# The residual's identity matmuls go first in each output tile of the gated mixer

## The chip, the cores and the metric

One core of one Trainium2 chip runs the whole program in one launch. The metric is the device time in microseconds of an execution; of several executions the median counts.

## What the kernel must compute

One inference step through two layers, for 1,024 prompt tokens and 64 sample tokens (8 sequences of 8), 1,088 tokens together. Layer 0 has a gated mixer in chunks of 128 tokens, layer 1 has sliding-window attention, and each is followed by a gated ConvFFN. The part that matters here is the end of the gated mixer with its residual:

```python
z = gelu(h @ w_in);  u, v = split(z);  v = layer_norm(v)
mixed = einsum('gts,bnsgc->bntgc', tril(w_s), v in chunks) + b_s
y = x + (u * mixed) @ w_out          # w_out is 2048 x 1024
```

Everything is f32. The kernel keeps activations with features on the 128 partitions and tokens along the free axis, so the residual x, which lies in memory by tokens, must be transposed where it is added.

## The kernel before, in words

All large products are computed from operands that are split in a high and a low part. A raw block of weights, `wraw`, is loaded by DMA from the SyncE queue (`load`, L295); ScalarE rounds it to `wh` (`hi`, L302), VectorE subtracts to get `wl` (`lo`, L306). Each of the three has two slots, s = 0 and s = 1. TensorE then does three products per block: weights high by activations high, high by low, low by high. `rows` (L323) does this for one block of 128 input features: nine matmuls, three products by three column chunks of 384, 384 and 320 tokens, which are added up in three PSUM banks. There are two such areas of three banks, A (banks 0 to 2) and B (banks 3 to 5); a tile m of an output uses area m % 2.

The gated mixer runs in three steps: v (`token_major`, L1734), u with the mixing matmuls (L323 and L1769), and the output projection, `out_tile`, which the change touches. The output projection has 8 tiles of 128 output features. A tile has 16 blocks `rows`, 8 on the weights of slot 0 and 8 on those of slot 1, on the gated product in its parts `gh` and `gl`. Between the two halves stands the residual: 9 matmuls in the program, one for each tile of tokens, whose stationary operand is the x of 128 tokens by 128 features, `xm`, and whose moving operand is the identity `idn`. So x comes out transposed and is added in PSUM to the sum. Both operands are f32, and each of these matmuls stands in the trace twice, 18 a tile, at L1788.

What orders the work around them:

- Semaphores alone, and the order in which each engine's program is written. TensorE waits on `free` (the area has been read out), on `w_lo` (the slot's weights are split), for tile 0 on `g_lo` before each block (that block of `gl` is there), and on `xm_in` (the residual's tile has landed). It signals `w_used` at the end of each half, on which the next split into that slot waits, and `xm_used` after the residual's matmuls, on which the next load of `xm` waits. There is one buffer `xm`.
- `gh` lies over the memory of the projections' input `hh` and `hl`, so ScalarE starts on it (L1181) only when TensorE has done the last u tile. VectorE first does the gating of the last group (L1439 to L1450) and then `gl` (L1468), 16 blocks, each after the `gh` of the block. Meanwhile TensorE does the last mixing matmuls (L1769) and comes to output tile 0.
- SyncE issues, for m = 0 to 6, the two weight loads of tile m + 1 (each waits for the split of the slot before), then waits for `xm_used` of tile m, and issues the two DMAs of `xm` for tile m + 1 (L988, L989).
- ScalarE, in each tile: the split of slot 0 for the next tile after the first half; after the second half the copy of the area to x (L1202), the split of slot 1, and the squares for the next norm (L1191), which GpSimd adds up (L1069).
- After tile 7 come the ConvFFN's first blocks (L323 on `hh`, `hl`), which wait for the scaled x in its two parts (L1212, L1484).

Of the kernel before, what the change touches and what calls it, by code (L numbers as in the profile page):

```python
# [12 lines left out]
TT = 9  # L13
# [65 lines left out]
def step_program(nc, x_prompt, x_sample, cache_swa_k, cache_swa_v, state_ffn_conv, mix_norm_g, sgu_w_in, sgu_ln_g,  # L79
# [7 lines left out]
    with ExitStack() as ctx:  # L87
        ctx.enter_context(nc.allow_non_contiguous_dma(reason="small vectors"))

        def sb(name, shape, dt=f32, stack=ctx):  # L90
            return stack.enter_context(nc.sbuf_tensor(name, shape, dt))

        def sem(name):
            return ctx.enter_context(nc.semaphore(name))


        idn = sb("idn", [128, 128])
# [6 lines left out]
        xm = sb("xm", [128, TT, 128])  # L104
# [108 lines left out]
        ps = ctx.enter_context(nc.psum_tensor("ps", [128, 8, 512], f32))  # L213
        BANK = (0, 3)
# [35 lines left out]
        g_hi, g_lo, xm_in, xm_used = sem("g_hi"), sem("g_lo"), sem("xm_in"), sem("xm_used")  # L250
# [38 lines left out]
        def at(c, m=0, i=None):  # L289
            return c if i is None else i * m + c  # L290
# [28 lines left out]
        def rows(pe, area, s, k, col, mov, start, stop):  # L319

            for n, (w, part) in enumerate(PARTS):
                for c, (c0, cn) in enumerate(CH):
                    ins = pe.matmul(ps[:, BANK[area] + c, 0:cn], w[:, s, col:col + 128], mov[part][:, k, c0:c0 + cn],  # L323
                                    start=start and n == 0, stop=stop and n == 2, skip_group_check=True)
            return ins
# [18 lines left out]
        x_mov, g_mov = (hh, hl), (gh, gl)  # L344
# [1315 lines left out]
        def _(pe):  # L1660
# [38 lines left out]
            for g in range(GROUPS):  # L1699
                ins = pe.transpose(ps[:, 5 + g // 4, (g % 4) * 128:(g % 4) * 128 + 128], wsr[:, g, :], idn[:, :])  # L1700
# [3 lines left out]
            for n in range(4):  # L1704
                ins = pe.transpose(ps[:, 7, 32 + 88 * n:120 + 88 * n], vecs[0:88, 1 + n, :], idn[0:88, 0:88])
# [45 lines left out]
            with pe.Fori(0, 8) as i:  # L1751
                for s in range(2):
# [5 lines left out]
                    for k in range(KT):  # L1758
                        ins = rows(pe, 0, s, k, 128 * k, x_mov, k == 0, k == 7)
# [3 lines left out]
                    for t in range(TT):  # L1763
                        n = 128 if t < 8 else 64
# [3 lines left out]
                        for r, (a, w) in enumerate(((vnh, src[0]), (vnh, src[1]), (vnl, src[0]))):  # L1768
                            ins = pe.matmul(o, a[:, t, :], w[:, gi, :].rearrange("p o n -> p (o n)"),  # L1769
                                            start=r == 0, stop=r == 2)  # L1770
# [3 lines left out]
            def out_tile(m, i=None):  # L1774
                area = m % 2
                pe.wait_ge(free[area], at((A_O, B_O)[area] + m // 2, 1, i))
                for s in range(2):
                    pe.wait_ge(w_lo, at(2 * (P_OUT + m) + s + 1, 4, i))
                    for k in range(8):
                        if m == 0:  # L1780
                            pe.wait_ge(g_lo, 8 * s + k + 1)
                        ins = rows(pe, area, s, 8 * s + k, 128 * k, g_mov, s == 0 and k == 0, s == 1 and k == 7)
                    ins.then_inc(w_used, 1)
                    if s == 0:
                        pe.wait_ge(xm_in, at(32 * (m + 1), 64, i))
                        for t in range(TT):
                            n = 128 if t < 8 else 64
                            ins = pe.matmul(ps[:, BANK[area] + t // 3, (t % 3) * 128:(t % 3) * 128 + n], xm[0:n, t, :],  # L1788
                                            idn[0:n, 0:n], start=False, stop=False, skip_group_check=True)
                        ins.then_inc(xm_used, 1)  # L1790

            by_pairs(pe, out_tile)

            def transpose_y(m):
# [100 lines left out]
            for m in range(KT):  # L1895
                ins = pe.transpose(ps[0:64, m // 4, (m % 4) * 128:(m % 4) * 128 + 128], x[:, m, SEQ:T], idn[:, :])
# [27 lines left out]
```

## Time and profile before

| | |
|---|---|
| three runs | 2893.01, 2893.94 (median), 2895.33 us |
| profiled execution, its time | 2889.9 us |
| profiled execution, its span | 2888.0 us |
| mean granted clock of TensorE | 0.971 |
| TensorE matmuls busy | 2765.0 us, 96% of the span |
| VectorE busy | 1500.1 us, 52% |
| ScalarE busy | 761.8 us, 26% |
| GpSimd busy | 158.3 us, 5% |
| DMA | 131.10 MB, mean 45 GB/s |

A granted clock of 1.00 is TensorE's upper level, 2.4 GHz; 0.50 is the lower, 1.2 GHz; a value between is a stretch with some of each. A matmul's duration in the trace is longer than its distance to the next, since they are pipelined: rates are read from starts.

### The profile page before, as it was taken

To read this page: it belongs to the slowest core of one execution; us is meant where nothing else is said; L and a number is where in the kernel's file an instruction comes from. 1 tells how busy PE (TensorE), PEld (TensorE's weight loads), DVE (VectorE), ACT (ScalarE), POOL (GpSimd) and SP (SyncE) were. 2 spreads that over 40 slices of the span, in tenths; PEclk is the share of its full clock that TensorE was granted. 3 is DMA by queue.
4 is the path that set the end of the run, shared out by engine and by line. 5 is a ranking of instruction groups with operands and counts; after the bars stand their busy time and mean duration, and the time that the engine had idled before them with its cause. 6 is when DMAs were issued, how large, how long until landed. Compare 5 with 4: busy or idle time off the path is not lost.

```text
span 2888.0 us, 44609 instructions
## 1 busy us (share of the span) xinstructions
PE 2765.0 (96%) x18002; PEld 2702.8 (94%) x18002; DVE 1500.1 (52%) x2168; ACT 761.8 (26%) x1219; POOL 158.3 (5%) x109
## 2 busy tenths in 40 slices
PE   8999999999999999999999967789999999999998
PEld 8999999998999999999998955479899999999998
DVE  5226666102655555555573299923555555555546
ACT  4112223112222222222233336512322222222221
POOL 0000000110000000000021043201100000000000
PEclk9999999999999999999999977879999999999999
DMA  4111111211111111111111100011111111111112
GB/s 139 38 54 46 40 46 55 63 57 45 41 42 45 45 45 45 45 45 44 41 39 52 36 35 1 20 30 37 38 45 44 39 43 45 45 45 45 45 45 70
DMA packets 192182, 131.10 MB, mean 45 GB/s; under 512 B 6132, under 2 KB 179020, under 8 KB 192076
## 3 DMA queue, kind: packets, MB, share of 16 engines
q1 hardware_dynamic: 181240, 124.26, 14.3%
q10 hardware_dynamic: 10868, 5.79, 0.7%
q8 instruction: 54, 0.88, 0.1%
q14 instruction: 20, 0.16, 0.0%
HBM read 123.85 MB, written 8.15 MB: 46 GB/s over the span
## 4 chain that ended last, share of the span: by engine, by line
PE 90%; DVE 6%; ACT 3%; issue 1%; DMA 0%; DVEq 0%; POOL 0%; SPq 0%; ACTq 0%; POOLq 0%
PE ps L323 71%; PE ps L1734 12%; PE ps L1769 2%; ACT pr L500 1%; PE ps L889 1%; PE ps L1681 1%; PE ps L1815 1%; DVE stt L655 1%; DVE hl L1484 1%; DVE sm L651 1%; PE ps L1788 1%; PE ps L906 0%; ACT sm L491 0%; PE ps L1822 0%; DVE x L1569 0%
## 5 line engine op out<-in xcount | busy, mean ns | idle before, releaser
L323 PE MATMUL ps<-hh,wh 128*128 128x384 f32 (+1 forms) x2688 | 598.8, 331 | 16.4 <-DVE hl L1484 9.1
L323 PE MATMUL ps<-hl,wh 128*128 128x384 f32 (+1 forms) x2688 | 595.2, 329 | 0.0
L323 PE MATMUL ps<-hh,wl 128*128 128x384 f32 (+1 forms) x2688 | 594.8, 329 | 0.0
L302 ACT ACTIVATE wh<-wraw 128x1024 fp32r<-128x1024 f32 x200 | 212.4, 1063 | 1193.0 <-PE ps L323 1056.3
L323 PEld LDWEIGHTS ps<-hh,wh 128*128 128x128 f32 x2688 | 459.7, 189 | 19.8 <-issue 10.8
L323 PEld LDWEIGHTS ps<-hh,wl 128*128 128x128 f32 x2688 | 461.5, 189 | 0.0
L323 PEld LDWEIGHTS ps<-hl,wh 128*128 128x128 f32 x2688 | 461.3, 189 | 0.0
L306 DVE TENSOR_TENSOR wl<-wraw,wh 128x1024 fp32r<-128x1024 f32 x200 | 247.7, 1239 | 390.6 <-ACT wh L302 389.0
L1509 DVE TENSOR_TENSOR a_sb<-ps,rbc 128x768 f32<-128x768 f32 x88 | 84.3, 958 | 556.7 <-PE ps L323 556.6
L1569 DVE TENSOR_TENSOR x<-x,ps 128x768 f32<-128x768 f32 x352 | 237.9, 717 | 99.3 <-PE ps L323 97.9
L1734 PE MATMUL ps<-wh,hh 128*128 128x256 f32 x936 | 267.5, 286 | 9.6 <-DVE x L1569 6.5
L1734 PE MATMUL ps<-wl,hh 128*128 128x256 f32 x936 | 266.3, 285 | 0.0
L1734 PE MATMUL ps<-wh,hl 128*128 128x256 f32 x936 | 266.2, 284 | 0.0
L323 PE MATMUL ps<-fh,wh 128*128 128x384 f32 (+1 forms) x1008 | 222.7, 329 | 4.5 <-DVE wl L306 4.5
L323 PE MATMUL ps<-fl,wh 128*128 128x384 f32 (+1 forms) x1008 | 222.6, 329 | 0.0
L323 PE MATMUL ps<-fh,wl 128*128 128x384 f32 (+1 forms) x1008 | 222.6, 328 | 0.0
L1734 PEld LDWEIGHTS ps<-wh,hh 128*128 128x128 f32 x936 | 181.2, 194 | 10.3 <-issue 6.7
L1734 PEld LDWEIGHTS ps<-wl,hh 128*128 128x128 f32 x936 | 181.3, 194 | 0.0
L1734 PEld LDWEIGHTS ps<-wh,hl 128*128 128x128 f32 x936 | 181.2, 194 | 0.0
L323 PEld LDWEIGHTS ps<-fh,wh 128*128 128x128 f32 x1008 | 171.8, 188 | 5.0 <-issue 5.0
L323 PEld LDWEIGHTS ps<-fh,wl 128*128 128x128 f32 x1008 | 172.7, 188 | 0.0
L323 PEld LDWEIGHTS ps<-fl,wh 128*128 128x128 f32 x1008 | 172.3, 188 | 0.0
(234 smaller groups left out, 3102.4 us busy)
## 6 DMA issues: line engine op xcount, KB each, us to landing
wraw<-in_ffn_w_up SPq DMA_DIRECT2D x88, 512.0 KB, 3.8
wraw<-in_ffn_w_down SPq DMA_DIRECT2D x44, 512.0 KB, 3.3
wraw<-in_sgu_w_in SPq DMA_DIRECT2D x32, 512.0 KB, 4.5
wraw<-in_sgu_w_out SPq DMA_DIRECT2D x16, 512.0 KB, 4.0
wraw<-in_attn_w_qkv SPq DMA_DIRECT2D x12, 512.0 KB, 3.6
xin<-in_x_prompt SPq DMA_DIRECT2D x8, 512.0 KB, 9.6
xm<-in_x_prompt SPq DMA_DIRECT2D x8, 512.0 KB, 3.7
wraw<-in_attn_w_o SPq DMA_DIRECT2D x8, 512.0 KB, 3.9
```

Of the source, the lines that this page charges most:

```text
L302: act.activation(wh[:, s, :], wraw[:, s, :], ACT.Copy).then_inc(w_hi, 1)
L306: dve.tensor_tensor(wl[:, s, :], wraw[:, s, :], wh[:, s, :].bitcast(f32), sub).then_inc(w_lo, 1)
L323: ins = pe.matmul(ps[:, BANK[area] + c, 0:cn], w[:, s, col:col + 128], mov[part][:, k, c0:c0 + cn], start=start and n == 0, stop=stop and ...
L500: act.activation(pr[:, z, 128 * h:128 * h + 128], sm[:, z, 128 * h:128 * h + 128], ACT.Exp, bias=stt[:, 8 * z + h:8 * z + h + 1], scale=HD ...
L651: ins = dve.copy_predicated(sv[:, e], tb2[:, C_CUR:C_CUR + 128].bitcast(i32).unsqueeze(1).to_broadcast([128, 2, 128]), ps[:, b + e, 0:256] ...
L655: dve.reduce_max(stt[:, 48 + 4 * z:52 + 4 * z], sm[:, z, :].rearrange("p (h n) -> p h n", h=4), AX.X).then_inc(s_mrg, 1)
L889: ins = pe.matmul(o, qm[64 * e:64 * e + 64, 2 * g + j, 64 * b:64 * b + 64], kcT[64 * e:64 * e + 64, b, (g - e) % NKV, :], start=b == 0, st ...
L1484: dve.scalar_tensor_tensor(hl[:, k, :], x[:, k, :], gains[:, col + k:col + k + 1], hh[:, k, :].bitcast(f32), mult, sub).then_inc(h_lo, 1)
L1509: dve.tensor_tensor(a_sb[:, z, 2:770].rearrange("p (c n) -> p c n", c=2), ps[:, b:b + 2, 0:384], rbc[:, 0:768].rearrange("p (c n) -> p c n ...
L1569: ins = dve.tensor_tensor(dst, dst, src, add)
L1734: ins = pe.matmul(o, a[:, 4 * s + k, TOK0[t]:TOK0[t] + 128], w[:, s, 256 * k:256 * k + 256], start=s == 0 and k == 0 and n == 0 and t % 2 ...
L1769: ins = pe.matmul(o, a[:, t, :], w[:, gi, :].rearrange("p o n -> p (o n)"), start=r == 0, stop=r == 2)
```

## The change

In `out_tile` the wait for `xm_in`, the nine identity matmuls and the signal `xm_used` move from between the two halves to the head of the tile, behind the wait for the area and ahead of the wait for weights. The identity matmuls now start the sums in their banks (`start` at the first of each bank), and the first block `rows` no longer does. No instruction, transfer or buffer is added or taken away.

```diff
             def out_tile(m, i=None):
                 area = m % 2
                 pe.wait_ge(free[area], at((A_O, B_O)[area] + m // 2, 1, i))
+                pe.wait_ge(xm_in, at(32 * (m + 1), 64, i))
+                for t in range(TT):
+                    n = 128 if t < 8 else 64
+                    ins = pe.matmul(ps[:, BANK[area] + t // 3, (t % 3) * 128:(t % 3) * 128 + n], xm[0:n, t, :],
+                                    idn[0:n, 0:n], start=t % 3 == 0, stop=False, skip_group_check=True)
+                ins.then_inc(xm_used, 1)
                 for s in range(2):
                     pe.wait_ge(w_lo, at(2 * (P_OUT + m) + s + 1, 4, i))
                     for k in range(8):
                         if m == 0:
                             pe.wait_ge(g_lo, 8 * s + k + 1)
-                        ins = rows(pe, area, s, 8 * s + k, 128 * k, g_mov, s == 0 and k == 0, s == 1 and k == 7)
+                        ins = rows(pe, area, s, 8 * s + k, 128 * k, g_mov, False, s == 1 and k == 7)
                     ins.then_inc(w_used, 1)
-                    if s == 0:
-                        pe.wait_ge(xm_in, at(32 * (m + 1), 64, i))
-                        for t in range(TT):
-                            n = 128 if t < 8 else 64
-                            ins = pe.matmul(ps[:, BANK[area] + t // 3, (t % 3) * 128:(t % 3) * 128 + n], xm[0:n, t, :],
-                                            idn[0:n, 0:n], start=False, stop=False, skip_group_check=True)
-                        ins.then_inc(xm_used, 1)
```

## Rows read from the trace of the kernel before

**Rows 1.** The page, part 4: the chain that ended last, by engine.

```profile
PE 90%; DVE 6%; ACT 3%; issue 1%; DMA 0%; DVEq 0%; POOL 0%; SPq 0%; ACTq 0%; POOLq 0%
```

**Rows 2.** Stretches: us, engines' busy time, granted clock, DMA; output projection, attention.

```profile
473.00:690.60 217.60, 213.15 (x1298) 211.43 (x1297) 40.79 (x36) 46.89 (x59) 20.09 (x14) 0.98 0.20 57
...
1500.00:2080.00 580.00, 490.48 (x3652) 440.64 (x3651) 319.77 (x488) 222.31 (x594) 131.58 (x85) 0.87 0.10 31
```

**Rows 3.** The chain in order of time: start us, us, engine, line, count.

```profile
476.29 1.21 DVE gl L1468
477.64 14.41 PE ps L323 x72
...
494.20 24.19 PE ps L323 x144
```

**Rows 4.** Timeline of PE into tile 0: start, us, operation [idle before, releaser].

```profile
472.91 0.28 PE L1769 MATMUL ps<-wsh,vnl 128*128 x1
477.64 1.24 PE L323 MATMUL ps<-gh,wh 128*128 128x384 f32 x3 [4.45 <-DVE gl L1468]
478.68 1.11 PE L323 MATMUL ps<-gl,wh 128*128 128x384 f32 x3
...
482.31 0.74 PE L323 MATMUL ps<-gh,wl 128*128 128x384 f32 x3
482.89 0.66 PE L323 MATMUL ps<-gh,wh 128*128 128x384 f32 x3
```

**Rows 5.** Timeline of PE at the middle of tile 0.

```profile
491.89 2.31 PE L1788 MATMUL ps<-idn,xm 128*128 128x128 f32 x18
494.13 0.76 PE L323 MATMUL ps<-gh,wh 128*128 128x384 f32 x3
494.73 0.66 PE L323 MATMUL ps<-gl,wh 128*128 128x384 f32 x3
```

**Rows 6.** Short stretches around the stall (clock: third number from the end).

```profile
475.00:476.00 1.00, 0.00 (x0) 0.00 (x0) 1.00 (x1) 1.00 (x2) 0.00 (x0) 0.83 0.44 124
476.00:482.00 6.00, 4.36 (x14) 4.39 (x15) 6.00 (x6) 6.00 (x7) 0.00 (x0) 0.50 0.22 67
482.00:483.00 1.00, 1.00 (x6) 1.00 (x6) 1.00 (x2) 1.00 (x2) 0.00 (x0) 0.76 0.00 0
```

**Rows 7.** Timeline of PE at a shorter stall, early in the first ConvFFN.

```profile
703.44 0.76 PE L323 MATMUL ps<-hh,wh 128*128 128x384 f32 x3 [2.16 <-DVE hl L1484]
704.04 0.85 PE L323 MATMUL ps<-hl,wh 128*128 128x384 f32 x3
...
708.16 1.06 PE L1815 MATMUL ps<-idn,pst 16*128 16x16 f32 x8
```

**Rows 8.** Timeline of PE at another, late in that ConvFFN.

```profile
1486.93 0.60 PE L1822 MATMUL ps<-idn,stc 128*18 128x128 f32 x4
1489.76 0.73 PE L323 MATMUL ps<-fh,wh 128*128 128x384 f32 x3 [2.23 <-DVE wl L306]
1490.34 0.66 PE L323 MATMUL ps<-fl,wh 128*128 128x384 f32 x3
```

**Rows 9.** Timeline of ACT: the last readout of area A before tile 0.

```profile
470.29 1.14 ACT L1166 ACTIVATE u<-ps 128x768 f32<-128x768 f32 x2 [5.14 <-PE ps L323]
```

**Rows 10.** Timeline of DVE: the low parts, and the weight split for tile 2.

```profile
476.21 19.32 DVE L1468 TENSOR_TENSOR gl<-gt,gh 128x1088 fp32r<-128x1088 f32 x16
...
519.58 1.23 DVE L306 TENSOR_TENSOR wl<-wraw,wh 128x1024 fp32r<-128x1024 f32 x1 [9.81 <-ACT wh L302]
```

**Rows 11.** Timeline of SP's queue: issues, merged from the first to the last.

```profile
444.06 0.58 SPq L988 DMA_DIRECT2D xm<-in_x_prompt  x1
...
522.24 14.51 SPq L295 DMA_DIRECT2D wraw<-in_sgu_w_out  x2
546.90 0.37 SPq L988 DMA_DIRECT2D xm<-in_x_prompt  x1
```

**Rows 12.** The page, part 6: issues of `xm`, KB each, median us to landing.

```profile
xm<-in_x_prompt SPq DMA_DIRECT2D x8, 512.0 KB, 3.7
```

## The prediction, made before the changed kernel was run

> **What bounds the kernel now.** I read the chain of waits first, then busy time by stage, then the timeline around the stage that the diff touches. The chain lies on TensorE for 90% [rows 1], so only what shortens TensorE's own time, or a wait of TensorE, can move the end. In the output projection TensorE is busy 213.15 of 217.60 us at a mean clock of 0.98 [rows 2]; the stage has one wait, 4.45 us before tile 0. The last mixing matmul ends at 472.91 + 0.28 = 473.19, and the first block of tile 0 starts at 477.64 [rows 4]. The chain says why: VectorE's first low part of the gated product runs from 476.29 for 1.21 us, and TensorE is on the chain from 477.64 [rows 3]. The lasting effect of the stall is in the clock. The granted clock falls to the lower level within 475 to 476, stays at 0.50 from 476 to 482 and is back within 482 to 483 [rows 6]. Six groups of three matmuls from 477.64 to 482.89 take 5.25 us [rows 4]. At full clock such a group takes 0.60 us behind identity work or a wait (494.13 to 494.73 [rows 5], the same from 703.44 to 704.04 [rows 7]) and 0.50 otherwise: the chain has 144 matmuls, 48 groups, in 24.19 us [rows 3]. At the upper level the six would take 0.60 + 5 x 0.50 = 3.10, so the low clock costs 2.15 us. Stall and clock together are 6.6 us, 0.23% of the time.
>
> **The change part by part.** *The identity block of tile 0.* It takes 494.13 - 491.89 = 2.24 us (18 records, 124 ns each), and the group behind it 0.60 in place of 0.50 [rows 5]: 2.34 us on the path. After the change it can start when the mixing is done, 473.19: its area A was read out by 470.29 + 1.14 = 471.43 [rows 9], and its x was issued at 444.06 [rows 11], with 3.7 us to landing [rows 12], so neither wait holds it. It ends at about 475.4, 2.2 us before the low part that ends the stall. The start of the first weight block stays at 477.64, for that is set by VectorE, whose gating and low parts read area B and wait for nothing that the identities do. So the whole 2.34 us go: they lie beside VectorE's work. If this cover were gone (low parts ready at 473.2) the block would cost the same 2.34 at the head as in the middle, and the change would give nothing. The bounds of this term are 0 and 2.34; the row is direct, and I take 2.34.
>
> In a sentence by itself: the Trainium skill (TensorE: Matmul & The Clock Gate, Back-to-back issue gap) gives about 81 ns for each matmul of 128 columns in a stream of weight loads and matmuls, by which the block would be an estimated 18 x 0.081 = 1.46 us and this term 1.46 in place of 2.24. The trace does not agree for f32 operands, 124 ns, and the trace's figure is the one in the sum.
>
> *What is late next in tile 0.* VectorE makes 16 low parts in 19.32 us, 1.21 each [rows 10]; TensorE uses one in 9 matmuls, three groups of 0.50, 1.50 us. It starts behind the first and falls back by 0.29 a block, so the low parts never stop it, even with the identities gone from the middle: the ninth is ready at 476.2 + 9 x 1.21 = 487.1 and is wanted after 477.6 + 12 = 489.6 at the earliest.
>
> *The clock.* The stall of 4.45 us becomes about 2.2 us of identity matmuls and 2.2 us of idling. The trace has two stalls of just this length. At 2.16 us before 703.44 the clock fell: the six groups from there to 708.16 take 4.72 in place of 3.10, a loss of 1.62 [rows 7]. At 2.23 us before 1489.76 it did not: the next group comes after 0.58 [rows 8]. So the loss of 2.15 in tile 0 becomes 1.62 or 0, a gain of 0.5 or 2.15. Ends of the range: 0 (the low stretch stays as it is) and 2.15. I take the fall with its 1.62, hence a gain of 0.53, because the row of 703.44 is the nearer in kind: same engine wait on a low part, with dense f32r blocks to either side; the other differs only in that small f32 work stands ahead, which the new order has too, so I give it nearly as much.
>
> *Tiles 1 to 7.* There the identities only change places. They cost 2.34 before and after: both orders have one passage into f32 and one out of it per tile. The operands' waits: the second weight load of a pair is the last of SyncE's work before the wait for `xm_used`; for tile 3 it is issued by 522.24 + 14.51 = 536.75, and tile 3's x was issued at 546.90, behind the identities in mid-tile [rows 11]. Now x follows the weights directly, at about 536.8, and lands 3.7 us later [rows 12], at 540.5. A tile is 24.19 + 2.15, or 26.3 us, long (the chain counts the identities' passage of 0.10 with the blocks); tile 1 begins at about 494.13 + 12.1 = 506.2, tile 3 at 558.9, so x is 18 us early. SyncE has nothing else queued behind this wait but the next slot-0 weights, which wait for the split at 519.58 + 1.23 [rows 10] of the tile, later than the moved signal in every tile; they are not held up. The signal for slot 0, `w_used`, comes 2.34 us later within its tile, but its slot is wanted again 2.34 us later too, behind the next tile's identities: the distance stays a half tile of 12 us plus the block, while the split needs from 494.20 + 24.19 = 518.39 [rows 3] to 519.58 + 1.23 = 520.81 [rows 10], 2.4 us. Slot 1 has the same distance before and after. The split of tile 1's first slot waits on VectorE for the low parts to end at 476.21 + 19.32 = 495.5 and is done at 495.5 + 1.2 = 496.7 [rows 10], 6 us ahead of tile 1 even when that starts 3 us earlier. Terms: 0 each; bounds +0.1 and -0.1 us a tile, for a semaphore wait whose place in the stream is new (the 0.10 of the passage is the nearest row).
>
> *Sum.* -2.34 - 0.53 + 0 = -2.9 us against the profiled execution: 2889.9 to 2887.0. What follows tile 7 is started by its end, by semaphores, so it moves with it. The median of the runs is 4.0 above the profiled execution, and I carry the difference over: 2893.94 - 2.9 = 2891.0 us.
>
> **The rivals.** (a) The clock stays up through the short idle time: gain 2.34 + 2.15 = 4.5, 2889.4 us. For it speaks the 2.23 us stall without a fall [rows 8], against it the 2.16 us one [rows 7]. (b) No gain: 2893.9. Either the identities do not run in the stall, because something holds them to the end of it (the readout of A and the landing of x are both done, which speaks against), or the gain is lost to other stretches of low clock later. (c) Slower: the same count of low parts and stalls follows at new moments, above all in attention, whose mean clock is 0.87 over 580 us [rows 2], so 0.26 x 580 = 150 us at the lower level. A stall of 2.2 us fell in one place and not in another, so an earlier start may turn some of its stalls that now pass into ones that fall, each at about 1.6 us [rows 7]. Two more such stretches than before eat the gain, three give 2895.9 - 0.1; from six on it is slower by over 0.2%. Against it: the same shift may save as many. The three runs, which presumably differ just so, span 2.3 us. (d) Residual late at the head of a tile: it would need a landing 18 us slower than 3.7, the price then would be up to seven times the lateness; not seen anywhere in the rows.
>
> **How the numbers follow.** Forecast (gain of 2 to 3.7) 0.45; (a) 0.25; (b) 0.15; (c) 0.13; (d) 0.02. Gains over 5.8 us (0.2%, about what can be told from no change) need (a) and a good turn of the later stalls, or more than I see: 0.11. Slower by over 0.2% is the far end of (c) and (d): 0.04. The rest, 0.85, is within. The range reaches from 2888.0, (a) with a little more, to 2894.5, the near end of (c).
>
> **What would show it.** In the changed kernel's trace the 18 identity records of tile 0 stand right behind the mixing matmuls, the wait before the first block falls from 4.45 to about 2.2 us, that block still starts 1.3 us behind the start of the first low part, and the two halves of a tile follow at 0.50 a group with nothing between. From the first block to the end of tile 0 it should be 2.34 + 0.5 us shorter (4.5 in case (a)), and tiles 1 to 7 the same 26.3 us. The prediction is wrong if tiles become longer or shorter by over 0.1, if `xm` becomes a releaser of TensorE, or if the stages behind differ by more than a few low-clock stretches.

## The result: faster by 7.8 to 8.7 us, about three times the 2.9 us of the forecast

| comparison | before, median | changed, median | ratio, 95% interval |
|---|---|---|---|
| first, 9 runs each | 2894.96 us | 2886.27 us (2880.25 to 2891.20) | 0.9969, 0.9959 to 0.9980 |
| second, 21 and 11 runs | 2893.76 us | 2885.96 us (2880.23 to 2889.19) | 0.9975, 0.9966 to 0.9984 |

The forecast was 2891.0 us with a range of 2888.0 to 2894.5. The measured median lies below it. The gain is 0.3%, and both intervals lie clear of 1. The single executions of the changed kernel spread over 11 us; the 94 executions of the kernel before in all four comparisons, less one far out at 2923.8, have a mean of 2893.5, and all but seven of them lie between 2892.2 and 2897.1. The profiled execution of the changed kernel, 2880.43 us with a span of 2878.5, is one of its fastest. The one of before, 2889.9, was fast for its kernel as well.

**Tile 0.** The timeline of PE of the changed kernel answers to [rows 4, 5]: start, us, operation, and in brackets the idle time before and what ended it.

```profile
473.23 0.28 PE L1769 MATMUL ps<-wsh,vnl 128*128 x1
473.34 2.39 PE L1780 MATMUL ps<-idn,xm 128*128 128x128 f32 x18
477.95 0.73 PE L323 MATMUL ps<-gh,wh 128*128 128x384 f32 x3 [2.22 <-DVE gl L1468]
478.52 0.66 PE L323 MATMUL ps<-gl,wh 128*128 128x384 f32 x3
479.02 0.66 PE L323 MATMUL ps<-gh,wl 128*128 128x384 f32 x3
```

The 18 identity records stand right behind the mixing, the stall is 2.22 us instead of 4.45, and then the groups of three follow at 0.57 and 0.50 us: full rate from the first. The short stretches around it, against [rows 6], show the granted clock (third number from the end) at 1.00 throughout:

```profile
475.00:476.00 1.00, 0.73 (x6) 0.47 (x4) 0.97 (x3) 1.00 (x2) 0.00 (x0) 1.00 0.31 91
476.00:482.00 6.00, 4.05 (x24) 4.08 (x25) 6.00 (x6) 6.00 (x7) 0.00 (x0) 1.00 0.57 167
482.00:483.00 1.00, 1.00 (x8) 1.00 (x7) 1.00 (x2) 1.00 (x2) 0.00 (x0) 1.00 0.09 16
```

The chain in order of time, against [rows 3], has tile 0 in one piece; the tiles behind it are 528.52 - 502.18 = 26.34 us long, as before.

```profile
476.60 1.21 DVE gl L1468
477.95 24.23 PE ps L323 x144
502.18 2.15 PE ps L1780 x18
504.33 24.19 PE ps L323 x144
528.52 2.15 PE ps L1780 x18
```

**Behind the output projection.** To see where the rest came from, I took the blocks at which TensorE comes out of a long wait; each appears once in every profile. These are the lines of the kernel before, the first profiled execution (timeline of PE):

```profile
715.65 0.76 PE L323 MATMUL ps<-hh,wh 128*128 128x384 f32 x3 [1.41 <-ACT rbc L1230]
1697.41 1.09 PE L810 MATMUL ps<-idn,qr 128*128 128x128 f32 x4 [12.26 <-DVE qr L603]
1929.22 1.11 PE L897 MATMUL ps<-idn,ssc 64*128 64x64 f32 x8 [8.07 <-DVE ssc L752]
1951.38 1.24 PE L323 MATMUL ps<-hh,wh 128*128 128x384 f32 x3 [3.41 <-DVE hl L760]
2052.92 1.25 PE L323 MATMUL ps<-hh,wh 128*128 128x384 f32 x3 [2.77 <-DVE hl L1484]
2073.17 0.76 PE L323 MATMUL ps<-hh,wh 128*128 128x384 f32 x3 [1.41 <-ACT rbc L1230]
```

and of the changed kernel:

```profile
689.32 0.73 PE L323 MATMUL ps<-hh,wh 128*128 128x384 f32 x3 [2.77 <-DVE hl L1484]
709.94 0.76 PE L323 MATMUL ps<-hh,wh 128*128 128x384 f32 x3 [1.41 <-ACT rbc L1230]
1484.05 0.73 PE L323 MATMUL ps<-fh,wh 128*128 128x384 f32 x3 [2.23 <-DVE wl L306]
1691.55 1.08 PE L810 MATMUL ps<-idn,qr 128*128 128x128 f32 x4 [12.26 <-DVE qr L603]
1922.39 1.11 PE L897 MATMUL ps<-idn,ssc 64*128 64x64 f32 x8 [8.08 <-DVE ssc L752]
1944.54 1.25 PE L323 MATMUL ps<-hh,wh 128*128 128x384 f32 x3 [3.40 <-DVE hl L760]
2044.98 0.73 PE L323 MATMUL ps<-hh,wh 128*128 128x384 f32 x3 [2.77 <-DVE hl L1484]
2065.24 0.76 PE L323 MATMUL ps<-hh,wh 128*128 128x384 f32 x3 [1.41 <-ACT rbc L1230]
```

The waits in the brackets are the same to 0.01 us, and what differs is the work between them. The table takes the differences of the starts. It uses 693.53 and 1489.76 of the first profile too, and a second profiled execution of the kernel before that the experiments brought (b2: last fence of the next section, and the starts 716.61, 1956.63, 2058.02 and 2078.27):

| stretch | before, 1st | before, 2nd | changed |
|---|---|---|---|
| start to tile 0 | 477.64 | 478.20 | 477.95 |
| tile 0 to first ConvFFN | 215.89 | 216.29 | 211.37 |
| its first blocks | 22.12 | 22.12 | 20.62 |
| its loop | 774.11 | 774.13 | 774.11 |
| its end and QKV | 207.65 | 210.82 | 207.50 |
| attention | 231.81 | 232.92 | 230.84 |
| attention, last part | 22.16 | 22.15 | 22.15 |
| attention's output projection | 101.54 | 101.39 | 100.44 |
| second ConvFFN, first blocks | 20.25 | 20.25 | 20.26 |
| to the end | 814.83 | 814.83 | 813.26 |
| span | 2888.0 | 2893.1 | 2878.5 |

Three things are to be seen. The dense stretch of 774 us is the same in all. The output projection gave 215.89 - 211.37 = 4.52 us, or 4.92 against the second profile. And five later stretches, in which no instruction was changed, come in two or three distinct lengths, 1 to 3 us apart; the changed kernel's profile has all five at the short end.

The difference is low clock. In the first blocks of the first ConvFFN the granted clock (third from the end) is 0.85 before and 1.00 in the changed kernel:

```profile
693.53:715.65 22.12, 18.55 (x87) 16.97 (x87) 10.16 (x8) 11.94 (x15) 3.42 (x3) 0.85 0.09 25
689.32:709.94 20.62, 15.77 (x87) 13.89 (x87) 10.17 (x8) 11.95 (x15) 3.42 (x3) 1.00 0.09 27
```

In the last stretch the kernel before has one more stall of 2.2 us, the counterpart of the one in [rows 8] in the second ConvFFN, and there the clock fell (granted 0.50 from 2848 to 2851), while behind the changed kernel's same stall, at 2839.35, it stayed at 1.00:

```profile
2847.29 0.73 PE L323 MATMUL ps<-fh,wh 128*128 128x384 f32 x3 [2.24 <-DVE wl L306]
2847.86 1.05 PE L323 MATMUL ps<-fl,wh 128*128 128x384 f32 x3
```

The traces also hold the start and the end of each time at the lower level (a fall and the next rise). Summed by stretch, the time at the lower level in the five stretches was 6.8, 23.7, 91.9, 6.0 and 6.0 us before, 6.8, 26.4, 96.4, 5.8 and 6.2 in the second profile, and 0, 23.7, 90.9, 3.2 and 2.3 in the changed kernel: it is larger wherever a stretch is clearly longer.

### The profile page after: what moved, and what is told of

Its sections match the earlier page's. It is cut to its first block, busy times and chain, and to the rows that moved or that the text cites. A ratio compares the mean times of both kernels' runs of the same rounds, so it can differ in the third digit from the quotient of the medians.

```text
span 2878.5 us, 44610 instructions
## 1 busy us (share of the span) xinstructions
PE 2757.1 (96%) x18002; PEld 2695.7 (94%) x18002; DVE 1499.9 (52%) x2168; ACT 762.0 (26%) x1219; POOL 158.4 (6%) x109
## 4 chain that ended last, share of the span: by engine, by line
PE 90%; DVE 5%; ACT 2%; issue 1%; DMA 0%; DVEq 0%; POOL 0%; SPq 0%; ACTq 0%; POOLq 0%
PE ps L323 71%; PE ps L1734 12%; PE ps L1769 2%; PE ps L889 1%; PE ps L1681 1%; ACT pr L500 1%; PE ps L1814 1%; DVE stt L655 1%; DVE sm L651 1%; DVE hl L1484 1%; PE ps L1780 1%; PE ps L906 0%; PE ps L1821 0%; ACT sm L491 0%; DVE x L1569 0%
```

## The experiments

Each ran against the kernel before on the same chip within one comparison; e1 to e4, e5 to e8, and r2, e10, e9 and b2 are three comparisons, on three chips. "Own work" below is what the edit itself takes off or puts on TensorE's path; means are of the single executions, each less the mean of before in its comparison (one execution of e8 at 2922.1 us is left out). These mean differences are uncertain (one standard error) by 0.6 to 1.2 us, that of e1 by 1.8. By them the full change is 8.9 us below in the first comparison (uncertain by 1.4) and 8.0 in the second (1.2).

**e1: the identities first in tile 0 alone.**

The nine identity matmuls with their wait and signal stand in a helper `residual()` here, against the changed kernel:

```diff
+                first = m == 0
...
+                if first:
+                    residual()
...
+                    if s == 0 and not first:
+                        residual()
```

> The identities go first in tile 0 alone; tiles 1 to 7 keep them in the middle. Theory A (all of the gain comes from tile 0: the block hidden in the stall, 2.34 us, the low clock behind the stall avoided, up to 2.15, and later stalls met at another moment of the clock): same gain as the full change, 6 to 10 us, ratio 0.9965 to 0.998. Theory B (part of it comes from tiles 1 to 7, from the earlier transfer or the undivided halves): a gain of 2.3 to 4.5 us, the rest missing.

Measured: 2887.86 us median of 7 (2880.14 to 2891.69), ratio 0.9976 (0.9965 to 0.9987), mean 7.7 us below before. Its profiled span is 2878.3 us, with 211.38 us from tile 0 to the ConvFFN: the full change's. With a mean uncertain by 1.8 us the time alone would hardly exclude theory B; the profile and e2 do.

**e2: the identities first in tiles 1 to 7 alone.**

```diff
+                first = m > 0
```

> The identities go first in tiles 1 to 7 alone; tile 0 keeps them in the middle. Theory A: no change, within 1 us of the kernel before, and the wait ahead of tile 0 is 4.45 us as before. Theory B: faster by 2 to 6 us.

Measured: 2893.28 us, ratio 1.0000 (0.9991 to 1.0009), mean difference 0.0; the stall is 4.45 us. Tiles 1 to 7 contribute nothing that can be told (uncertain by 0.6), and neither does the earlier transfer of `xm`.

**e3: the rest of the stall filled.**

```diff
+                first = True
...
+                if m == 0:
+                    for _ in range(8):
+                        pe.matmul(ps[:, 6, 0:128], idn[:, :], idn[:, :], start=True, stop=True)
```

> The full change, and 8 more identity matmuls (16 records, about 2.0 us) into an unused PSUM bank behind the residual's of tile 0, so that TensorE idles about 0.2 us there in place of 2.2. Nothing is computed from them. Theory A: the start of the first weight block stays, the clock of tile 0 stays at 1.00 in every execution. If the low clock behind the 2.2 us rest of the stall still costs up to 1.6 us in some executions of the full change, this is faster than the full change by 0 to 1.6 us and varies less; else it is the same.

Measured: 2888.74 us, ratio 0.9981 (0.9972 to 0.9990), mean 5.5 us below. The stall was 0.24 us and tile 0 to ConvFFN took 211.36 us, no better than the full change's profile. Its later stretches came out long (22.04, 209.27, 232.91, 101.40, 814.82 by the same starts), and its span is 2886.9. So the two profiles differ by 8.4 us although tile 0 to the ConvFFN is the same: 7.8 of it lie in the five later stretches, and 0.6 ahead of tile 0, which starts at 478.57 here.

**e4: only the idling filled, order as before** (17 of those matmuls ahead of tile 0, and `first = False`).

> The order of before in every tile, and 17 extra identity matmuls (34 records, about 4.2 us) into an unused PSUM bank in the stall of 4.45 us ahead of tile 0: only the idling is taken away, no work leaves the path. Theory A: tile 0 gains 2.15 us from the clock and nothing from the block, so 2.15 us plus or minus what later stalls do with the clock (0 to 4 us more): 2 to 6 us faster. If the clock had no part in the gain: no change.

Measured: 2892.00 us, ratio 0.9992 (0.9983 to 1.0001), mean 2.2 us below (uncertain by 0.8). The time alone is hardly clear of no change; the profile carries the reading. Tile 0 to ConvFFN is 213.71 us, 2.18 less than the 215.89 of before and 2.58 less than the 216.29 of b2. So the low clock behind the stall cost 2.2 to 2.6 us by itself, and the hidden block is what the full change has beyond it, 213.71 - 211.37 = 2.34 us.

**e5: everything behind the projection 4.5 us earlier by leaving work out,** stall kept. 18 identity matmuls are not done, so part of the residual is missing.

```diff
-                        for t in range(TT):
+                        for t in range({1: 8, 6: 8, 7: 2}.get(m, 0), TT):
```

> The order of before in every tile, but 18 of the identity matmuls are left out (the residual of 8 token tiles in output tiles 1 and 6, of 2 in tile 7, is not added): 36 records, 4.5 us less work on TensorE, with the stall and the low clock of tile 0 kept. So everything behind the output projection comes 4.5 us earlier, as in the full change, by another way. Theory A (later stalls cost low clock by the moment at which they come): the time falls by as much as with the full change, 7 to 9 us, to about 2885.5. Theory C (the later gain belongs to the warm tile 0 or to the order itself, not to the moment): 4.5 us, 2889.2.

Measured: 2888.18 us, ratio 0.9970 (0.9952 to 0.9988), mean 6.2 below, between the two theories. The work left out was smaller than planned: tile 0 to ConvFFN is 690.25 - 478.14 = 212.11 us, 3.8 to 4.2 below the two profiles of before. The profiled execution is short in the ConvFFN's first blocks (20.59), long everywhere behind.

**e6: the full change, with 18 matmuls put on the path in tile 6.**

```diff
+                for _ in range(18 if m == 6 else 0):
+                    pe.matmul(ps[:, 6, 0:128], idn[:, :], idn[:, :], start=True, stop=True)
```

> The full change, and 18 extra identity matmuls into an unused PSUM bank in the dense work of tile 6: 4.5 us more on TensorE, so that everything behind the output projection comes at the moment it had before the change. Theory A: the whole gain goes, also its later part: the time of before, 2893 to 2894. Theory C: the full change plus 4.5 us, 2890 to 2891.

Measured: 2891.88 us, ratio 0.9981 (0.9962 to 0.9999), mean 2.9 below, in three clusters: 3 executions near 2885, 3 near 2891, 6 near 2893.3. The 36 records took 4.0 us (215.39 - 211.37), 112 ns each, not 4.5. Theory A's strict form falls here. This timeline of its PE is at the moment of before, 693.46 against 693.53, with the same first wait, and yet keeps to the short length, 714.06 - 693.46 = 20.60 us. In the kernel before the clock was low from 694.1 to 697.5 (which is also why its wait ahead of 703.44 is 2.16 and not 2.57 us) and again from 704.3 to 707.8 [rows 7]; the stretch was 1.5 us longer by the two together.

```profile
693.46 0.74 PE L323 MATMUL ps<-hh,wh 128*128 128x384 f32 x3 [2.77 <-DVE hl L1484]
697.57 0.76 PE L323 MATMUL ps<-hh,wh 128*128 128x384 f32 x3 [0.88 <-DVE hl L1484]
703.39 0.76 PE L323 MATMUL ps<-hh,wh 128*128 128x384 f32 x3 [2.57 <-DVE hl L1484]
714.06 0.76 PE L323 MATMUL ps<-hh,wh 128*128 128x384 f32 x3 [1.41 <-ACT rbc L1230]
```

So the moment in the kernel's own time, counted from its start, doesn't decide. What does is taken up under "What stays open".

**e8: the same with 9 matmuls.**

> The full change, and 9 of those matmuls in tile 6: 2.2 us. Theory A: the later stalls come at a third moment; the time is anything from the full change plus 0 to the full change plus 6 us, and its later stages show another pattern of low clock than either kernel. Theory C: the full change plus 2.2 us, 2888.2.

Measured: 2890.49 us, ratio 0.9988 (0.9962 to 1.0015), mean 3.8 below. Its profile is the most instructive. The code up to tile 5 is the full change's, and so is the stall, and here the clock falls behind it. First the timeline of PE, then stretches with the granted clock third from the end:

```profile
477.92 0.74 PE L323 MATMUL ps<-gh,wh 128*128 128x384 f32 x3 [2.22 <-DVE gl L1468]
...
478.99 0.79 PE L323 MATMUL ps<-gh,wl 128*128 128x384 f32 x3
479.58 1.11 PE L323 MATMUL ps<-gh,wh 128*128 128x384 f32 x3
...
482.30 0.87 PE L323 MATMUL ps<-gh,wh 128*128 128x384 f32 x3
```

```profile
479.00:480.00 1.00, 1.00 (x7) 1.00 (x6) 1.00 (x1) 1.00 (x2) 0.00 (x0) 0.68 0.69 184
480.00:482.00 2.00, 2.00 (x8) 2.00 (x7) 2.00 (x3) 2.00 (x3) 0.00 (x0) 0.50 0.04 11
482.00:483.00 1.00, 1.00 (x5) 1.00 (x5) 1.00 (x2) 1.00 (x2) 0.00 (x0) 0.62 0.06 16
```

Groups at 0.91 us in place of 0.50. Tile 0 to ConvFFN took 214.90 us: 211.37, plus 2.0 for the 18 records, plus 1.5 for this fall. The 2.22 us stall therefore does both, without a fall in the profiles of the full change (twice), e1 and e6, with one in e8.

**e7: later stalls filled too.**

```diff
                         if first:
+                            for _ in range(10 if k == 0 else 7 if k == 4 and L == 0 else 0):
+                                pe.matmul(ps[:, 6, 0:128], idn[:, :], idn[:, :], start=True, stop=True)
                             pe.wait_ge(h_lo, 8 * (0 if L == 0 else 3) + k + 1)
...
                     if m == 0:
+                        for _ in range(12 if k == 0 else 0):
+                            pe.matmul(ps[:, 6, 0:128], idn[:, :], idn[:, :], start=True, stop=True)
                         pe.wait_ge(h_lo, 16 + k + 1)
```

> The full change with the rest of the stall ahead of tile 0 filled, and with identity matmuls into an unused PSUM bank in later stalls of TensorE too: 10 ahead of the first block of each ConvFFN (stall 2.77 us), 7 ahead of the fifth block of the first ConvFFN (2.2 to 2.6 us), 12 ahead of the attention's output projection (3.4 us). Nothing is computed from them. Theory A: the low clock behind these stalls goes (1.5, 1.6, 2.4 and 1.3 us in the profiled kernel before) whatever the moment: faster than the full change by 1 to 4 us, 2882 to 2885, and less spread between executions; what the attention stage does stays open. Theory C: no more than the full change.

Measured: 2885.86 us, ratio 0.9966 (0.9948 to 0.9984), mean 7.6 below: no better than the full change, so theory A missed, but spread over 7.7 us in place of 11. The stretch it left alone, the ConvFFN's end and QKV, was 210.83 us in its profile.

**r2: the full change again.**

> The full change again, as its own comparison. Theory D (the moment at which the clock changes its level differs between executions, and each of the five stretches behind tile 0 comes out short or long by it): single executions again between 2880 and 2891, mean 6 to 9 us below the kernel before. Theory E (the first comparison of the full change drew lucky executions; only tile 0's 4.5 us are real): mean 3.5 to 5.5 us below.

Measured: the second line of the result table; mean 8.0 below. Its profile repeats the first one's lengths within 0.2 us (211.37, 20.59, 207.40, 230.79, 100.44). Theory E would have needed 5.5 us at most, against 8.0 (uncertain by 1.2) and 8.9 in the first comparison: the size is real.

**e10: the kernel before with 18 matmuls put on the path in tile 6.**

> The kernel before with 18 extra identity matmuls into an unused PSUM bank in the dense work of tile 6, 36 records, 4.0 us at the 112 ns each measured for them; everything behind comes 4.0 us later, stall and low clock of tile 0 as before. If the kernel before sits at an unfavourable moment for the later stalls, as theory D with a tie between the low clock of tile 0 and what follows has it: less than 4.0 us slower, 1 to 3. If the moment makes no difference on average (E): 4.0 us slower, 2897.5.

Measured: 2894.40 us, ratio 1.0006 (0.9997 to 1.0015), mean 1.8 us above (uncertain by 0.9), though 4.0 us of work were added: the rest, about half, was taken back behind. The stretch ahead of the attention was 207.42 us in its profile.

**e9: most long stalls filled.**

```diff
                 pe.wait_ge(f_lo, J + 2 * FI)
+                for _ in range(8):
+                    pe.matmul(ps[:, 6, 0:128], idn[:, :], idn[:, :], start=True, stop=True)
...
+            pe.wait_ge(halo, 4 * FI)
+            for _ in range(25):
+                pe.matmul(ps[:, 6, 0:128], idn[:, :], idn[:, :], start=True, stop=True)
             for a in (0, 1):
                 pe.wait_ge(free[a], (A_WO, B_WO)[a])
-            pe.wait_ge(halo, 4 * FI)
...
             ins.then_inc(stat, 1)
+            for _ in range(13):
+                pe.matmul(ps[:, 7, 0:128], idn[:, :], idn[:, :], start=True, stop=True)
```

> As the kernel with the later stalls filled, and with 8 more identity matmuls ahead of the last down projection of each ConvFFN (stall 2.23 us), 25 ahead of the QKV projection (6.5 us) and 13 behind its statistics (3.2 us). Nothing is computed from them. Theory D: the stretch from the ConvFFN's end to the attention, 207.4 us at its shortest and 210.8 in the kernel with fewer fillers, keeps to the short length: 1 to 4 us faster than that kernel, 2882 to 2885, a version that beats the full change. Rival: fillers in stalls that other engines end do not come back, since those waits are fixed: same as that kernel, 2886.

Measured: 2881.28 us (2878.46 to 2883.64, 5 runs), ratio 0.9961 (0.9947 to 0.9975), 4.7 us below the full change of the same comparison by the medians and 3.9 (uncertain by 1.4) by the means, with 5 executions: the fastest version. Theory D holds. The first two lines of its PE's timeline give the filled stretch, 1691.03 - 1484.97 = 206.06 us, under the shortest seen without fillers, 207.40.

```profile
1484.97 0.73 PE L323 MATMUL ps<-fh,wh 128*128 128x384 f32 x3 [0.45 <-DVE wl L306]
1691.03 1.09 PE L814 MATMUL ps<-idn,qr 128*128 128x128 f32 x4 [12.26 <-DVE qr L603]
...
1940.99 5.29 PE L924 MATMUL ps<-idn 128*128 128x128 f32 x24 [0.69 <-ACT qkv L556]
1946.04 0.74 PE L323 MATMUL ps<-hh,wh 128*128 128x384 f32 x3
```

The last two lines show fillers that were too long, taken over from e7. The 12 ahead of the attention's output projection met the low clock (granted 0.50 from 1940 to 1946) and took 5.05 us for 24 records, so the first block came 24.48 us behind the block at L897 (L901 here, 1921.56), against 22.15 in the changed kernel. The next stretch was shorter by 1.5 us (98.92 for 100.44); e7 lost 2.1 us in the same place. Against the changed kernel's profile these 12 cost more than they saved.

**b2: the kernel before again, one profiled execution.**

> The kernel before again, one profiled execution. Theory D: most executions of it take 2892 to 2896 us while the first profiled one took 2889.9, so this one, if it is an ordinary one, shows more of the five stretches at their long length: 209.3 for 207.65 us ahead of the attention and 232.9 for 231.8 in it; the times up to tile 0 and of tile 0 stay.

Measured: 2894.95 us, an ordinary execution, span 2893.1. Lines of its PE's timeline:

```profile
478.20 1.24 PE L323 MATMUL ps<-gh,wh 128*128 128x384 f32 x3 [4.45 <-DVE gl L1468]
694.49 0.73 PE L323 MATMUL ps<-hh,wh 128*128 128x384 f32 x3 [2.77 <-DVE hl L1484]
1490.74 1.11 PE L323 MATMUL ps<-fh,wh 128*128 128x384 f32 x3 [2.23 <-DVE wl L306]
1701.56 1.09 PE L810 MATMUL ps<-idn,qr 128*128 128x128 f32 x4 [12.26 <-DVE qr L603]
1934.48 1.11 PE L897 MATMUL ps<-idn,ssc 64*128 64x64 f32 x8 [8.07 <-DVE ssc L752]
```

All five stretches are at their long end: 210.82 and 232.92 where the first profile had 207.65 and 231.81. At 1490.74 the same 2.23 us stall as in [rows 8] is followed by a group of 1.11 us, a fall; in the first profile there was none.

## Why the prediction was right in the block, and wrong in the clock and in what follows tile 7

- *The identity block, 2.34 us.* Right. It runs in the stall, the first weight block still starts with VectorE's first low part (1.35 us after its start, as before), and between e4 and the full change lie 213.71 - 211.37 = 2.34 us.
- *What is late next in tile 0.* Right: no wait of TensorE on `gl` after the first.
- *Tiles 1 to 7, no change.* Right: 26.34 us, and e2 measured 0.0.
- *The clock in tile 0.* The step said "I take the fall with its 1.62, hence a gain of 0.53". This failed, by size. The gain was 2.2 us or more in four profiles and about 0.65 in e8's. I wrote "The trace has two stalls of just this length", one with a fall and one without, and read them as a difference of kind between the two places. The same trace held a third, 2.24 us at 2847.29, of the very kind that I had as the one without, and there the clock fell. Second profiles show that each place can go either way: e6 against before at 703.4 (there the wait was 2.57 us, since no fall had come ahead of it), b2 against before at 1490. My rival (a) was the likelier case, and its 4.5 us is the part of the gain that belongs to the output projection.
- *What follows tile 7 "moves with it".* This is the step that failed most. The sum has no term for it. It moved in order and in waits, but its work took 3.5 to 4.4 us less in the mean: 8.0 to 8.9 us in all, about 4.5 of it up to tile 7. Rival (c) had the mechanism, stretches of low clock that depend on when the stalls are reached, but I looked there only for a loss. For a gain I had "the same shift may save as many" and, for all gains over 5.8 us, a chance of 0.11. A kernel whose later stretches were nearly all at their long end had little to lose and much to gain.
- *"The median of the runs is 4.0 above the profiled execution, and I carry the difference over."* The number held, but the profile of before was as fast as the fastest seven of the 94 executions. An ordinary one, b2, is 5.1 us longer, of which 3.17 and 1.11 lie in two later stretches. Had I taken the difference of 4.0 us as a question, it would have led to the falls behind tile 7.
- *The spread.* I wrote that the three runs span 2.3 us and used that as the size of what the clock could do. The changed kernel's executions span 11 us.

**What stays open.** Behind tile 7 every version but e4 ended below the sum of its own work: the full change by 3.5 to 4.4 us, e1 by 3.2, e5 by about 2, e6 by 2.4, e8 by 1.3, e3 by 1.0, e10 by 2.2, e4 by 0, each uncertain by about 1 (e1 by 1.8). So the kernel before sits near the unfavourable end.

Why a given stall falls in one execution and not in another can be read from the profiles, though no run was made for it. TensorE starts each execution at the lower level: its matmuls at L1681 start 0.21 us apart until the clock's first rise, then 0.12. That rise came at 14.9 us in the first profile of before and at 16.3 in b2 (timelines of PE, then b2's granted clock around its stall, to hold against [rows 6]):

```profile
14.49 0.41 PE L1681 MATMUL ps<-wh,hh 128*128 128x256 f32 x1
14.71 0.36 PE L1681 MATMUL ps<-wl,hh 128*128 128x256 f32 x1
14.90 0.28 PE L1681 MATMUL ps<-wh,hl 128*128 128x256 f32 x1
```

```profile
16.07 0.41 PE L1681 MATMUL ps<-wh,hl 128*128 128x256 f32 x1
16.28 0.31 PE L1681 MATMUL ps<-wh,hh 128*128 128x256 f32 x1
16.43 0.28 PE L1681 MATMUL ps<-wl,hh 128*128 128x256 f32 x1
```

```profile
477.00:478.00 1.00, 0.00 (x0) 0.00 (x0) 1.00 (x2) 1.00 (x2) 0.00 (x0) 0.57 0.80 240
...
483.00:484.00 1.00, 1.00 (x5) 1.00 (x4) 1.00 (x2) 1.00 (x2) 0.00 (x0) 0.52 0.00 0
```

The fall ahead of tile 0 began at 475.65 in the one and at 477.14 in the other, 2.5 and 3.4 us after the last mixing matmul had ended, and in both 460.8 us behind the first rise; so it did in e2, e5 and e10. The fall is tied to the first rise and not to the start of the stall, and in b2 it lasts further into tile 0 and costs 0.4 us more. The other places agree. Counted from the first rise, tile 0 started behind its 2.22 us stall at 462.2 to 462.5 us in the four profiles without a fall and at 462.8 in e8. The block behind the 2.77 us stall of the first ConvFFN started at 672.9, 674.7, 678.2 to 678.7 and 682.4 in the six profiles with a fall (e3, e4, b2, before, e2, e10), and at 673.5 to 674.3 and 677.6 to 677.7 in the six without (the full change twice, e1, e5, e6, e8). That is what parts before from e6, whose starts are alike (693.53 and 693.46) and whose rises are not (14.9 and 15.9). At the 2.23 us stall near 1490 the falls are at 1467.6, 1471.0 and 1474.4 (e7, e4, b2), the rest at 1468.3 to 1469.1, 1472.3 to 1472.4, 1474.9 and 1478.6.

What sets the first rise is open, and so is why the mean over executions favours the changed kernel. The rise came at 14.8 to 16.3 us in ten profiles and at 17.0 to 18.1 in the four whose program has fillers ahead of tile 0 (e3, e4, e7, e9), and a later rise also delays tile 0 itself: 477.64 us at 14.9, 478.20 at 16.3, 479.15 at 18.1 (e4). This may be why e3, with the same lengths through tile 7 as the full change, averaged 2.5 us more (uncertain by 1.1), and why e4 shows nothing behind its own work; with one profile of each it is not shown.

## What to carry to other kernels

Work that needs nothing from a late producer belongs in the wait for it; its worth is its own time on the path (2.34 us here) plus the low clock that the shorter stall avoids (2.2 to 2.6 where it avoids the fall). Where stalls of about 2 us stand in a TensorE-bound kernel, price each by both outcomes of the clock and take at least two profiles before one of them is called typical. Filling such stalls with matmuls of no use into a free PSUM bank gave a further 4 to 5 us here (e9; e7, with fewer places filled, gave nothing more than the full change). Size the fillers for the lower clock: where they met it, a record took 0.21 us in place of 0.11, and 12 of them outlasted their wait and delayed the next block by 2.3 us.

## What the runs showed of the hardware

- Equal stalls do not have equal consequences. 2.22 us ahead of tile 0: no fall in four profiles, one in a fifth. 2.23 us ahead of 1490: a fall in b2, e4 and e7, none in the ten others. A fall may also begin 1.4 us after TensorE has resumed (e8). The Trainium skill (TensorE: Matmul & The Clock Gate, Part 1) says that the activity monitor runs freely of the kernel, so that the same kernel shows a varying number of slow matmuls. The traces agree: the two profiles of before have their first rise at 14.9 and 16.3 us, and the falls shift with it.
- f32 identity matmuls of 128 columns took 124 ns each as the residual's and 112 ns with `idn` for both operands (4.0 us for 36 records) at the upper level, and the latter 210 ns at the lower (5.05 us for 24, e9).
- Unchanged stretches came out in steps, not in a smear: 20.6 or 22.1, 100.4 or 101.4, 813.3 or 814.8 us.
